# Prompt attention in pairs of heads, turned against a diagonal of reciprocal sums, with lags of one and two steps

## The reference, cut to what matters

```python
def softmax_stats(s):
    m = jnp.max(s, axis=-1, keepdims=True)
    e = jnp.exp(s - m)
    den = jnp.sum(e, axis=-1, keepdims=True)
    return e / den, (m + jnp.log(den))[..., 0]
...
    def block(args):
        qn, qr, i = args
        s = (jnp.einsum('bqhd,bkhd->bhqk', qn, k_nope)
             + jnp.einsum('bqhr,bkr->bhqk', qr, k_rope)).astype(jnp.float32) * scale
        qpos = i * Q_BLOCK + jnp.arange(Q_BLOCK)
        s = jnp.where(kpos[None, :] <= qpos[:, None], s, NEG_INF)
        p, _ = softmax_stats(s)
        return jnp.einsum('bhqk,bkhd->bqhd', p.astype(v.dtype), v)
```

## Time and profile before

| | us |
|---|---|
| median of 3 runs | 1352.41 (1345.26 to 1355.83) |
| profiled execution, its own time | 1351.47 |
| its span in the trace | 1349.7 |
| PE busy | 1258.1 (93%) |
| DVE busy | 592.2 (44%) |
| ACT busy | 485.9 (36%) |
| prompt attention, first score product to first product of the page stage | 152.19 |

### The profile page before, as it was taken

One profiled execution on the slowest core, in us unless ns is written; L12 is line 12 of the kernel. 1 busy time (PEld: TensorE's weight loads), 2 busy tenths in 40 slices (PEclk: granted clock), 3 DMA queues, 4 the chain that ended last, 5 costly groups with the idle time before them and its releaser, 6 DMA issues.

```text
span 1349.7 us, 21707 instructions
## 1 busy us (share of the span) xinstructions
PE 1258.1 (93%) x8308; PEld 1031.6 (76%) x8308; DVE 592.2 (44%) x1095; ACT 485.9 (36%) x861; POOL 45.6 (3%) x60
## 2 busy tenths in 40 slices
PE   4999989999999999999999869699999999999798
PEld 3997977333566466766677559599999999999698
DVE  4223221453675436666666464633333222334543
ACT  4232243111454336555555342333332122222332
POOL 0000000232000000000000000000000000000000
PEclk8999999866799669999999889799999999999899
DMA  6774413002348116777777402156464454562122
GB/s 239 250 250 141 143 39 95 0 0 85 125 157 288 63 28 194 237 231 238 237 239 238 133 32 95 47 203 217 155 217 156 140 198 160 203 213 97 58 79 86
DMA packets 68817, 202.68 MB, mean 150 GB/s; under 512 B 7457, under 2 KB 40226, under 8 KB 67394
## 3 DMA queue, kind: packets, MB, share of 16 engines
q1 hardware_dynamic: 66562, 131.74, 30.2%
q0 software_dynamic: 2176, 69.90, 14.5%
HBM read 196.53 MB, written 72.13 MB: 199 GB/s over the span
## 4 chain that ended last, share of the span: by engine, by line
PE 89%; DVE 8%; ACT 2%; issue 1%; DMA 0%; SPq 0%; DVEq 0%; ACTq 0%
PE ps L494 49%; PE ps L1005 13%; PE ps L387 4%; PE ps L953 4%; PE ps L973 4%; PE ps L398 3%; PE ps L962 2%; PE ps L410 2%; DVE R L435 2%; PE ps L1062 1%; DVE tmp L452 1%; PE ps L1056 1%; PE ps L917 1%; DVE aLo L353 1%; PE ps L1021 1%
## 5 line engine op out<-in xcount | busy, mean ns | idle before, releaser
L494 PE MATMUL ps<-aHi,wHi 128*128 128x272 f32 (+1 forms) x1392 | 295.9, 294 | 39.7 <-DVE aLo L353 36.3
L494 PE MATMUL ps<-aHi,wLo 128*128 128x272 f32 (+1 forms) x1392 | 291.5, 291 | 0.0
L494 PE MATMUL ps<-aLo,wHi 128*128 128x272 f32 (+1 forms) x1392 | 291.0, 291 | 0.0
L494 PEld LDWEIGHTS ps<-aHi,wHi 128*128 128x128 f32 (+1 forms) x1392 | 220.1, 189 | 49.7 <-issue 19.9
L366 DVE TENSOR_TENSOR wLo<-ring,wHi 128x1024 fp32r<-128x1024 f32 (+3 forms) x105 | 133.4, 1271 | 210.9 <-ACT wHi L361 210.8
L494 PEld LDWEIGHTS ps<-aLo,wHi 128*128 128x128 f32 (+1 forms) x1392 | 221.2, 190 | 0.0
L494 PEld LDWEIGHTS ps<-aHi,wLo 128*128 128x128 f32 (+1 forms) x1392 | 219.9, 190 | 0.0
L361 ACT ACTIVATE wHi<-ring 128x1024 fp32r<-128x1024 f32 (+3 forms) x105 | 114.5, 1091 | 196.1 <-PE ps L494 196.0
L1284 DVE TENSOR_REDUCE ssq<-att 128x8 f32<-128x512 f32 x128 | 87.4, 683 | 89.1 <-ACT att L748 88.2
L748 ACT ACTIVATE att<-ps 128x512 f32<-128x512 f32 x128 | 76.4, 597 | 114.3 <-PE ps L1005 113.8
L1005 PE MATMUL ps<-wkHi,pgHi 128*128 128x512 f32 x256 | 103.2, 403 | 8.2 <-ACT att L748 7.0
(11 more groups left out here) (181 smaller groups left out, 1535.9 us busy)
## 6 DMA issues: line engine op xcount, KB each, us to landing
out_o_cv<-in_cv POOLq DMA_DIRECT2D x16, 2044.0 KB, 8.3
ring<-in_wgu SPq DMA_DIRECT2D x44, 512.0 KB, 3.5
big<-in_pgt SPq DMA_DIRECT2D x128, 144.0 KB, 2.2
big<-in_pgl SPq DMA_DIRECT2D x128, 128.0 KB, 2.4
kv<-in_ck SPq DMA_DIRECT2D x8, 1792.0 KB, 8.5
ring<-in_win SPq DMA_DIRECT2D x21, 512.0 KB, 4.5
kv<-in_cv SPq DMA_DIRECT2D x8, 1024.0 KB, 5.7
kv<-in_cv SPq DMA_DIRECT2D x24, 256.0 KB, 6.0
```

The costliest lines, as they stand in the source:

```text
L494: ins = nc.tensor.matmul(pair[rows, a, 0:HT], w[:, c], xx[:, k, a * HT:(a + 1) * HT], start=(k == 0 and z == 0), stop=(k == nk - 1 and z = ...
```

## The change

Heads are taken in pairs: 32 units (p, i), each with the work of heads 2p and 2p+1 (z = 0, 1). Scores of the two go to the two halves of one pair of banks, `ps0` and `ps3` in turn. The probabilities are no longer multiplied by the reciprocal sums. Instead DVE forms a diagonal matrix for each head (identity times reciprocal, `dg`, 128x256 for the two), and the turn becomes a real product of the probabilities with that diagonal. One ACT copy takes both heads' turned blocks. Value products alternate between the heads. The turn runs one step behind the scores (`LAG_T`) and the value products two (`LAG_PV`). DVE runs at step n first mask and maximum of unit n, then reciprocal and diagonal of unit n-1. The two extra pieces, now at steps 24 and 26, take their turn in the alternation of `ps0` and `ps3`, and the DVE work on them stands ahead of the masks of those steps.

```diff
@@ constants and buffers
+LAG_T, LAG_PV = 1, 2
-        pr = att
+        prHigh = at("prHigh", [P, 2, 512], o_split + 4096 * 4)
-        prT = at("prT", [P, 2, 512], o_split + 5120 * 4)
+        prT = (at("prT", [P, 2, 512], o_split + 5120 * 4), ring[:, :, 1024:1536])
+        dg = tf[:, 512:1024].rearrange("p (a z n) -> p a z n", a=2, z=2)
-        units = [(h, i) for h in range(2 * H) for i in range(4)]
+        units = [(p, i) for p in range(H) for i in range(4)]
+        def probs_of(u, z):
+            k = 2 * (u % 3) + z
+            return att[:, k, :] if k < 4 else prHigh[:, k - 4, :]
-        ABSORB = 48
+        ABSORB, NEW = 24, 26
+        def score_pair(x):
+            return ps[0] if x % 2 == 0 else ps[3]
...
@@ scalar
-            for n in range(len(units) + 4):
-                if n >= 4:
-                    m = n - 4
...
+            for n in range(len(units) + LAG_T):
+                if n < len(units):
+                    w = (units[n][1] + 1) * P
+                    act.wait_ge(a_nm, n + 1)
+                    for z in range(2):
+                        pr = probs_of(n, z)[:, 0:w]
+                        last = act.activation(pr, pr, ACT.Exp, bias=st[:, n % 3, NEGM, z:z + 1],
+                                              accum_out=st[:, n % 3, SUM, z:z + 1])
+                    last.then_inc(a_e, 1)
+                if n >= LAG_T:
+                    m = n - LAG_T
                     w = (units[m][1] + 1) * P
                     act.wait_ge(a_t, m + 1)
                     if m >= 2:
                         act.wait_ge(a_pv, m - 1)
-                    act.activation(prT[:, m % 2, 0:w], ps[1][:, m % 2, 0:w], ACT.Copy).then_inc(a_tc, 1)
+                    act.activation(prT[m % 2][:, :, 0:w], ps[1][:, :, 0:w], ACT.Copy).then_inc(a_tc, 1)
...
@@ tensor
+            for n in range(len(units) + LAG_PV):
+                if n == ABSORB:
+                    absorb()
+                if n == NEW:
+                    new_scores()
                 if n < len(units):
+                    p, i = units[n]
+                    score_room(place(n))
+                    for z in range(2):
+                        q, k, _v = heads(2 * p + z)
+                        mm(score_pair(place(n))[:, z, 0:(i + 1) * P], q[:, i * P:(i + 1) * P], k[:, 0:(i + 1) * P],
+                           start=True, stop=True).then_inc(a_s, 1)
+                if n >= LAG_T and n - LAG_T < len(units):
+                    m = n - LAG_T
+                    i = units[m][1]
                     pe.wait_ge(a_p, m + 1)
-                    if m >= 2:
-                        pe.wait_ge(a_tc, m - 1)
+                    if m:
+                        pe.wait_ge(a_tc, m)
                     for j in range(i + 1):
-                        last = pe.transpose(ps[1][:, m % 2, j * P:(j + 1) * P], pr[:, m % 4, j * P:(j + 1) * P], cm(C_ID))
+                        for z in range(2):
+                            last = mm(ps[1][:, z, j * P:(j + 1) * P], probs_of(m, z)[:, j * P:(j + 1) * P], dg[:, m % 2, z, :],
+                                      start=True, stop=True)
                     last.then_inc(a_t, 1)
-                if n >= 5:
-                    m = n - 5
+                if n >= LAG_PV:
+                    m = n - LAG_PV
...
                     for j in range(i + 1):
-                        last = mm(ps[2][r, (h // 2) % 2, i * P:(i + 1) * P], v[:, j, (h % H) * HD:(h % H + 1) * HD],
-                                  prT[:, m % 2, j * P:(j + 1) * P], start=(j == 0), stop=(j == i))
+                        for z in range(2):
+                            h = 2 * p + z
+                            last = mm(ps[2][z * HD:(z + 1) * HD, p % 2, i * P:(i + 1) * P],
+                                      heads(h)[2][:, j, (h % H) * HD:(h % H + 1) * HD],
+                                      prT[m % 2][:, z, j * P:(j + 1) * P], start=(j == 0), stop=(j == i))
...
@@ vector
+                if n < len(units):
+                    p, i = units[n]
+                    w = (i + 1) * P
+                    mask = (C_MA if p < HP else C_MB) + (3 - i) * P
+                    if n >= 3:
+                        v.wait_ge(a_t, n - 2)
+                    for z in range(2):
+                        v.wait_ge(a_s, 2 * n + z + 1)
+                        v.tensor_tensor_reduce(probs_of(n, z)[:, 0:w], score_pair(place(n))[:, z, 0:w], C[:, mask:mask + w],
...
+                    v.tensor_scalar(st[:, n % 3, NEGM, :], st[:, n % 3, MAXI, :], -1.0, None, ALU.mult).then_inc(a_nm, 1)
+                if 1 <= n <= len(units):
+                    m = n - 1
                     v.wait_ge(a_e, m + 1)
-                    link(v.reciprocal(st[:, 12 + k:13 + k], st[:, 4 + k:5 + k]))
-                    v.tensor_scalar(pr[:, k, 0:w], pr[:, k, 0:w], st[:, 12 + k:13 + k], None, ALU.mult).then_inc(a_p, 1)
...
+                    link(v.reciprocal(st[:, m % 3, REC1, :], st[:, m % 3, SUM, :]))
+                    v.tensor_tensor(dg[:, m % 2, :, :], cm(C_ID).unsqueeze(1).broadcast_to([P, 2, P]),
+                                    st[:, m % 3, REC1, :].unsqueeze(2).broadcast_to([P, 2, P]), ALU.mult).then_inc(a_p, 1)
...
```

More of the change, by code:

```diff
@@ L509, in sp_weight_loop @@
                     sp_weight(u0 + j, pairs[j, bass.ds(f, 1), :, :].rearrange("a p n -> p (a n)"), f * 2)
[L512 removed]
+        units = [(p, i) for p in range(H) for i in range(4)]
+        MAXI, NEGM, SUM, REC1 = range(4)
         def heads(h):
@@ L946, in _, with score_room @@
             pe.wait_ge(kn_sq, 1)
-            for n in range(len(units) + 5):
-                if n < len(units):
[L949 to L957, removed]
+            def score_room(x):
+                if x < 2:
+                    return
+                if x - 2 == A_PLACE:
+                    pe.wait_ge(p_all, 1)
+                elif x - 2 == N_PLACE:
+                    pe.wait_ge(p_nr, 1)
+                else:
+                    pe.wait_ge(a_sm, 2 * ([place(u) for u in range(len(units))].index(x - 2) + 1))
@@ new lines, in absorb, with new_scores @@
+            def absorb():
+                pe.wait_ge(s_wkt, 16)
+                pe.wait_ge(p_read, 1)
+                score_room(A_PLACE)
+                for c in range(KC):
+                    for h in range(H):
+                        o = (c * H + h) * NS
+                        last = mm(score_pair(A_PLACE)[:, 0, o:o + NS], wkT[:, h, c * P:(c + 1) * P], qg[:, h, :], start=True, stop=True)
+                last.then_inc(p_ab, 1)
+            def new_scores():
+                pair = score_pair(N_PLACE)
+                pe.wait_ge(p_all, 1)
+                pe.wait_ge(q_ab, 2)
+                score_room(N_PLACE)
+                for k in range(KC):
+                    mm(pair[0:NS, 1, 0:256].rearrange("p (b n) -> p b n", b=NB), uT[:, U_LAT + k, NP_:T],
+                       qaAll[:, :, k * 32:(k + 1) * 32], start=(k == 0), stop=(k == KC - 1))
+                mm(pair[0:NS, 1, 256:512].rearrange("p (b n) -> p b n", b=NB), uT[MID, U_KR, NP_:T],
+                   qrB[MID, :, NOPE:HQ], start=True, stop=True)
+                for c in range(HP):
+                    last = mm(pair[0:NS, 0, 0:256].rearrange("p (b n) -> p b n", b=NB), uT[:, U_KS + c, NP_:T],
+                              qwS[:, :, c, :], start=(c == 0), stop=(c == HP - 1))
+                last.then_inc(p_new, 1)
@@ L972, in _ @@
                     for j in range(i + 1):
-                        last = mm(ps[2][r, (h // 2) % 2, i * P:(i + 1) * P], v[:, j, (h % H) * HD:(h % H + 1) * HD],
-                                  prT[:, m % 2, j * P:(j + 1) * P], start=(j == 0), stop=(j == i))
-                    last.then_inc(a_pv, 1)
-                if n == ABSORB:
-                    pe.wait_ge(s_wkt, 16)
-                    pe.wait_ge(p_read, 1)
-                    for c in range(KC):
-                        for h in range(H):
-                            o = (c * H + h) * NS
-                            last = mm(ps[3][:, 0, o:o + NS], wkT[:, h, c * P:(c + 1) * P], qg[:, h, :], start=True, stop=True)
-                    last.then_inc(p_ab, 1)
```

117 lines of the change are left out of this document (45 added, 72 removed).

## The result

The changed kernel takes 1382.89 us (median of 4 runs, 1379.61 to 1387.63) against 1352.72 us before (4 runs, 1345.26 to 1355.83): 30.2 us more, ratio 1.0235 with a 95% interval of 1.0191 to 1.0279: slower, though the interval leaves open whether by more than 2%. Its profiled execution took 1384.28 us, with a span of 1382.5.

The account below looks back on a forecast made before the run. PE's own time or its waits were taken as the bound. Stage: 155.7 us at 2.4 GHz + 4.3 + 11.5 for the clock = 171.5, 19.3 more than before; 1371.7 on the median's level, plus 1 us: 1373, range 1364 to 1387.

Parts of the forecast that it names:

- The wait: After each score group PE idles at the turn for DVE's diagonal: 1.37 to 1.77 us by width, some 40 us in all.
- A pair at 2.4 GHz: Two heads of prompt attention, PE's waits included, take 18.3 us at 2.4 GHz, where two heads took 14.6 before.
- the 8.7 us of extra pieces: Part of the old stage left for extra pieces and ends after 117.0 us of heads and 26.5 lost at 1.2 GHz.
- The products: Per pair, real turn products add 2.13 us in passes of 0.107; overlapping value products shrink from 4.27 to 2.13.
- The window scores: Window heads' half-row score products might overlap, 4.27 to 2.13 us per pair; no gain taken, since PE would only wait longer.
- The new tokens' block: DVE's 3.06 us block ahead of step 26's masks, with step 24's small copy: 2.7 us against 2.06, +0.6.
- The clock: TensorE's stretches at 1.2 GHz, where a pair loses 0.382 of its time: 4.3 us at the start, 11.5 in window heads.
- the start stays: The stage's first stretch at 1.2 GHz remains 11.3 us long and costs 4.3 us.
- for the way back: In window heads, turns and values in a row (3.4 and 1.3 us at 1.2 GHz) restore the clock within about a pair.
- Rival 1: Full-size turn products keep TensorE at 2.4 GHz after the start stretch: stage 160.0 us, total 1360; chance 0.15.
- Rival 2: Value products of the two heads don't overlap: 2.13 us more per pair, total 1390; chance 0.08.
- rival 5: The turn product costs one pass, or the diagonal far under 0.4 us: 17 us less at most, 1356; chance 0.03.

## Why the prediction was right, and where its size was off

The direction, the mechanism and the range hold; the time was 9.9 us too low (1373 against 1382.89), within the range and within the forecast's own, but that is a third of the 30.2 us lost. Step by step:

- **The wait.** Right in place and nearly in size. PE idles at the turn in 31 of 32 steps, 1.29 (256), 1.40 (384), 1.53 (512) and 1.23 to 1.44 us (128) in latent heads, released by L1285. "Some 40 us in all" was low, 52.4, for two reasons: window heads' scores run side by side and end earlier, so their waits are longer (1.71 at 256, 1.98 at 384), and the wait behind the new tokens' block is 4.14. The 1 us added in case DVE's pieces of preparation delay a mask has nothing for it in the trace: behind two fills of 0.91 us each, from 387.30 on, the next wait is 1.31, where a pair earlier it was 1.29. The lag and the order on DVE were each shown to remove it.
- **A pair at 2.4 GHz.** 18.3 forecast, 18.85 found. By steps from one score group to the next: 4.09, 4.41, 5.63 and 4.73 for widths of 256, 384, 512 and 128, against 3.94, 4.29, 5.50 and 4.56. The turn and value groups with their changes take 0.40 more per pair, nearly all of it the 0.10 by which each of the four turns is longer behind a wait; the chain of the diagonal takes 0.17. Over 8 pairs that is 4.4 us. One reading of the kernel before was mixed: of the four heads from 380.08 only three are latent (7.95, 6.81 and 6.80 us), and the fourth is the first window head. That doesn't move the forecast much, since the 8.7 us of extra pieces were taken as what the heads leave.
- **The products.** A pass of the turn is 0.112, a little over the 0.107 forecast: the turn of 16 passes takes 1.98 until the values start (368.23 to 370.21) and that of 4 passes 0.64 (373.43 to 374.07). Values overlap in full: six products take 0.80 (370.21 to 371.01), what three took before (415.62 to 416.42 in the earlier trace rows). The diagonal measured 0.425, for which L1278's 0.416 stood in. The product's price of 17 us came out as 14.1 where PE bounds.
- **The window scores.** "I take nothing" was right for the time of this kernel, for the reason given: the overlap is there, and PE waits it away.
- **The new tokens' block.** 0.6 us more than before was forecast. The wait is 4.14, of which a step of that width (384) has 1.98 anyway, so the block is worth 2.2 where it was 2.06 and 2.7 was forecast.
- **The clock.** This is the term that was mis-sized: "two such stretches and a bit, 30 us in place of 47.8: 11.5", and "the start stays: 11.3 x 0.382 = 4.3". The start stretch was 20.9 us, two in the latent heads add 3.4 each, and six in the window heads hold 40.8 where 30 were taken; together 68.5 in place of 41.3. The excess, 27.2 x 0.382 = 10.4, with the 4.4 of the pairs makes 14.8, and the stage (186.4) missed 171.5 by 14.9. The argument "for the way back" took the clock as a matter of the window heads; the runs show that PE's waits bring it down in latent heads too. What hit the median is smaller, 9.9, since the rest of the profiled program was 1.4 us shorter, 1 us had been added, and it is one execution above its median.

The rivals: the clock didn't hold, nor fall for good. Rival 1 needed a clock that the waits leave alone, at 1360; with the waits filled the time is 1366. Rival 2 fails on the value rows above, rival 5 on the turn's two passes of 0.112 per product and the diagonal's 0.425. The rule of the Trainium skill ("TensorE: Matmul & The Clock Gate", Part 4, PE-mode transpose), by which a transpose does not count as PE activity as a matmul does, is contradicted here for float32 transposes: in the waits they held the clock, at 0.95 against a product's 0.96. That real products in all turns would hold it was a further step, taken in the prediction, and no run bears it out: all turns were products, and the clock fell to a mean of 0.82 beside the waits. The measurement decides.

A table of the stage shows how far the two terms carry (waits are PE's for DVE's diagonal or ACT's copy; time at 1.2 GHz is twice the missing part of the mean clock by the stage):

| kernel | stage, us | PE's waits, us | mean clock | at 1.2 GHz, us |
|---|---|---|---|---|
| changed | 186.4 | 52.4 | 0.82 | 67 |
| diagonal twice | 225.0 | 66.6 | 0.71 | 130 |
| a product in each wait | 165.2 | 21.0 | 0.96 | 13 |
| diagonal first | 128.1 | 15.3 | 0.92 | 20 |
| lags 2 and 3 | 122.2 | 13.0 | 0.94 | 15 |
| lags 2 and 3, copy first | 111.7 | 3.0 | 0.94 | 13 |
| turn by transpose | 188.2 | 51.7 | 0.63 | 139 |
| lags 2 and 3, copy first, transpose | 94.7 | 6.5 | 0.96 | 8 |

Take the waits and 0.382 of the time at 1.2 GHz from each stage, and from the third also its 32 x 0.85 us of useless work, and 108, 109, 112, 105, 104 and 104 us are left in the first six: nearly the same work, though their stages differ by up to 113 us. The last two, without the product, are left with 83 and 85; for them 0.382, worked out for turns that are products, is only an approximation.

## What to carry to other kernels

When a loop is made tighter by bringing a consumer one step nearer, look at what stands ahead of its producer in the other engine's queue: an operation whose inputs were long ready can be late only because it is issued behind the next step's work, and swapping two blocks on DVE was worth 58 us here. A wait on PE that recurs in each step is to be priced twice, as itself and by the clock that it takes from all other products; in the changed kernel the second price was half of the first (26 us beside waits of 52), and for the waits added by the second diagonal it was larger than they (24 beside 14). And a change that moves the time the wrong way may hold a gain: with the waits hidden, the same products give 0.9656 of the time before.

## What the hardware showed that was not expected

- Two products on rows 0 to 63 and 64 to 127 of the array, in float32 and from different weights, run side by side in full. In the changed kernel the scores of both window heads at 256 columns are one group, 0.70 us as for one such product before (453.57):

```profile
483.12 0.70 PE L1012 MATMUL ps<-big 64*128 64x256 f32 x4
```

and at 512 columns, in the kernel of lags 2 and 3 with copy first and transposes, two products take the time that one took before (1.12 in the earlier trace rows):

```profile
390.14 1.13 PE L1012 MATMUL ps<-big 64*128 64x512 f32 x4
```

- Products for different output halves overlap even when a few for the same half are issued in a row: no loss with two blocks per head, 0.27 us with three, 0.48 with four. No run here shows why.
- The clock fell in the latent heads beside waits of 1.2 to 1.5 us, none of them as long as the 2.06 us of the earlier trace rows, and rose again each time (393.20 to 396.60 is the first such stretch). With 0.85 us of each wait filled, by a product or by transposes, it was 1.00 from 351 to 420, all through the latent heads behind the start.
- Before the change 47.8 us of the window heads ran at 1.2 GHz though PE hardly waited; with the pairs and no waits it was 6.8 us (with the turn as a product), although one cause named in the prediction, the small products, stayed. The scores on half of the rows, the other cause named, now come side by side in pairs; whether that is what changed was not tried alone.
